# Layer 1's weight tiles fetched two by two: 1 MB transfers with 8192 B a partition in place of 512 KB with 4096 B

## The reference, cut to what matters

```python
def trunk_layer(x, start_pos, conv_buf, pool_buf, k_buf, v_buf, norm_g, w_in, ..., w_out):
    h = rms_norm(x, norm_g)
    proj = jnp.einsum('btd,de->bte', h, w_in)                 # 1024 -> 3200 columns
    a_val, a_glu, a_gate, b_val, b_gate, q, k, v, c_gate = jnp.split(proj, cuts, axis=-1)
    u = a_val * jax.nn.sigmoid(a_glu)
    c = layer_norm(causal_dwconv(concat(conv_buf, u), conv_w, conv_b), ln_g, ln_b)   # width 31
    ya = jax.nn.silu(c) * jax.nn.silu(a_gate)
    yb = multiscale_pool(concat(pool_buf, b_val), ...) * jax.nn.silu(b_gate)
    q, k = rope(rms_norm(q), pos), rope(rms_norm(k), pos)
    kk, vv = concat(k_buf, k), concat(v_buf, v)
    yc = dilated_attention(q, kk, vv, ...) * jax.nn.silu(c_gate)
    new_k, new_v = kk[:, -n_keep:], vv[:, -n_keep:]           # the cache, moved by one position
    return x + concat(ya, yb, yc) @ w_out, new_conv, new_pool, new_k, new_v
```

## Time and profile before

| | us |
|---|---|
| three runs | 398.08, 400.06, 397.24 |
| profiled execution, its own time | 398.96 |
| its span, first to last instruction | 397.1 |
| TensorE busy | 343.2 (86%) |
| VectorE busy | 232.3 (58%) |
| ScalarE busy | 100.1 (25%) |
| moved by DMA | 157.73 MB, mean 397 GB/s |

### The profile page before, as it was taken

One profiled execution on the slowest core, in us unless ns is written; L12 is line 12 of the kernel. 1 busy time (PEld: TensorE's weight loads), 2 busy tenths in 40 slices (PEclk: granted clock), 3 DMA queues, 4 the chain that ended last, 5 costly groups with the idle time before them and its releaser, 6 DMA issues.

```text
span 397.1 us, 4745 instructions
## 1 busy us (share of the span) xinstructions
PE 343.2 (86%) x1550; PEld 270.0 (68%) x1550; DVE 232.3 (58%) x530; ACT 100.1 (25%) x237; POOL 58.5 (15%) x110
## 2 busy tenths in 40 slices
PE   3897799998879859989958999999979867989990
PEld 2676578886557646578847888888747644658880
DVE  2603769759975996431013489978985997540110
ACT  4300013542523122411011011453352222230011
POOL 4007740003400011044001320000600002000000
PEclk9999989999969898999996999999978998989997
DMA  8999999999999999999999999999999999999982
GB/s 300 422 414 402 419 417 403 419 421 414 420 419 417 420 415 401 409 413 416 411 404 415 417 418 409 421 421 417 421 419 417 416 386 355 376 396 384 389 346 87
DMA packets 44329, 157.73 MB, mean 397 GB/s; under 512 B 6988, under 2 KB 20116, under 8 KB 44306
## 3 DMA queue, kind: packets, MB, share of 16 engines
q0 software_dynamic: 14624, 88.25, 54.5%
q10 hardware_dynamic: 14420, 41.52, 26.4%
q1 hardware_dynamic: 15262, 27.67, 18.7%
HBM read 140.23 MB, written 104.46 MB: 616 GB/s over the span
## 4 chain that ended last, share of the span: by engine, by line
PE 50%; DVE 14%; SPq 12%; DMA 10%; issue 5%; ACTq 4%; ACT 4%; DVEq 0%
PE pj L704 24%; PE pj L847 14%; SPq L491 11%; DMA kg<-in_cache_k_win 10%; DVE yc L1307 3%; PE psc L776 3%; PE ptr L622 3%; DVE ssc L1251 2%; ACTq L471 1%; PE ps L824 1%; ACTq L885 1%; DVE spsum_pad L1277 1%; DVE tok L1245 1%; DVE sc L1213 1%; PE ps L830 1%
## 5 line engine op out<-in xcount | busy, mean ns | idle before, releaser
L704 PE MATMUL pj<-hT,wt 128*128 128x264 f32 x800 | 195.5, 403 | 7.4 <-DVE hT L1162 5.0
L704 PEld LDWEIGHTS pj<-hT,wt 128*128 128x128 f32 x800 | 157.0, 200 | 39.7 <-issue 12.7
L1307 DVE SCALAR_TENSOR_TENSOR yc<-u_ext,par,yc 128x256 f32<-128x256 f32 x180 | 77.2, 480 | 3.8 <-DVE u_smp L1191 1.0
L847 PE MATMUL pj<-mix,wt 128*128 128x264 f32 x256 | 61.1, 395 | 0.0
L847 PEld LDWEIGHTS pj<-mix,wt 128*128 128x128 f32 x256 | 49.2, 195 | 8.4
L611 POOL DMA_DIRECT2D out<-in_cache_v_win x48 | 26.2, 553 | 143.3 <-issue 143.3
L1377 DVE TENSOR_TENSOR xT<-xT,pj 128x264 f32<-128x264 f32 x16 | 6.9, 430 | 55.2 <-PE pj L847 55.2
L611 POOL DMA_DIRECT2D out<-in_cache_k_win x48 | 26.4, 557 | 82.0 <-issue 82.0
L965 ACT ACTIVATE ex<-pj 128x264 f32<-128x264 f32 x22 | 8.6, 390 | 77.1 <-PE pj L704 44.0
L1245 DVE TENSOR_TENSOR tok<-kg,qb 128x1536 f32<-128x1536 f32 x10 | 17.6, 1758 | 4.2 <-DMA kg<-in_cache_k_win 3.7
L1189 DVE SCALAR_TENSOR_TENSOR u_ext<-ex,pj 128x256 f32<-128x256 f32 x6 | 2.5, 421 | 29.9 <-ACT ex L965 29.9
(11 more groups left out here) (187 smaller groups left out, 334.8 us busy)
## 6 DMA issues: line engine op xcount, KB each, us to landing
wt<-in_w_tiles ACTq DMA_DIRECT2D x62, 512.0 KB, 32.3
out<-in_cache_k_win POOLq DMA_DIRECT2D x24, 1080.0 KB, 44.4
out<-in_cache_v_win POOLq DMA_DIRECT2D x24, 1080.0 KB, 81.3
out<-in_cache_k_win POOLq DMA_DIRECT2D x8, 1200.0 KB, 72.0
out<-in_cache_v_win POOLq DMA_DIRECT2D x8, 1200.0 KB, 89.3
out<-in_cache_k_win POOLq DMA_DIRECT2D x16, 432.0 KB, 64.2
out<-in_cache_v_win POOLq DMA_DIRECT2D x16, 432.0 KB, 87.3
kg<-in_cache_k_win SPq DMA_DIRECT2D x32, 144.0 KB, 33.5
```

Of the source, the lines that this page charges most:

```text
L704: last = nc.tensor.matmul(pj[n % RING][:, 0:T], wt[:, g % WRING, k, :], hT[:, k, :], start=(k == 0), stop=(k == KD - 1))
L847: last = nc.tensor.matmul(pj[n % RING][:, 0:T], wt[:, g % WRING, k, :], mix[:, k, :], start=(k == 0), stop=(k == KD - 1))
L1307: last = V.scalar_tensor_tensor(out=yc[:, t, 0:SEQ], in0=x_w, scalar=par[:, ROW_CW + w * CT + t:ROW_CW + w * CT + t + 1], in1=yc[:, t, 0:S ...
```

## The change: single tiles up to the first of layer 1, pairs behind it

Tiles 34 to 65 lie in memory as 16 pairs, each partition's two rows of 4096 B side by side. One transfer fills two neighbouring slots of the ring with pieces of 8192 B. ACT issues it where it issued the odd tile, so the even tile of a pair is asked for one step later than before, and the even step issues nothing. TensorE waits for the even slot's semaphore for both tiles. SBUF, the schedules and the arithmetic stay.

```diff
+PAIRED_FROM = 34
+assert PAIRED_FROM % 2 == WRING % 2 == DEPTH * NRING % 2 == 0
...
+PAIR_BYTES = 2 * KD * P * 4
...
-    tiles = np.stack(cols, axis=1).reshape(DEPTH, NRING, KD, P, P)
-    return tiles.transpose(0, 1, 3, 2, 4).reshape(DEPTH, NRING, P, KD * P)
+    tiles = np.stack(cols, axis=1).reshape(DEPTH * NRING, KD, P, P).transpose(0, 2, 1, 3).reshape(DEPTH * NRING, P, KD * P)
+    pairs = tiles[PAIRED_FROM:].reshape(-1, 2, P, KD * P).transpose(0, 2, 1, 3).reshape(-1, P, 2 * KD * P)
+    return tiles[:PAIRED_FROM], pairs
...
         def tile_of(g):
-            return wt[:, g % WRING, :, :].rearrange("p k c -> p (k c)"), ins["w_tiles"][g // NRING, g % NRING], w_in[g % WRING]
+            if g < PAIRED_FROM:
+                return wt[:, g % WRING, :, :].rearrange("p k c -> p (k c)"), ins["w_tiles"][g], w_in[g % WRING]
+            return wt[:, g % WRING:g % WRING + 2, :, :].rearrange("p t k c -> p (t k c)"), ins["w_pairs"][(g - PAIRED_FROM) // 2], w_in[g % WRING]
+
+        def tile_landed(g):
+            g -= g % 2 if g >= PAIRED_FROM else 0
+            return w_in[g % WRING], 16 * (g // WRING + 1)
...
-                        pe.wait_ge(w_in[g % WRING], 16 * (g // WRING + 1))
+                        pe.wait_ge(*tile_landed(g))
...
             def next_tile(g):
-                if g < DEPTH * NRING:
+                if g < PAIRED_FROM:
                     buf, src, landed = tile_of(g)
                     act.dma_start(buf, src).then_inc(landed, 16)
+                elif g < DEPTH * NRING and g % 2:
+                    buf, src, landed = tile_of(g - 1)
+                    act.dma_start(buf, src, max_dma_last_dim=PAIR_BYTES).then_inc(landed, 16)
```

More of the change, by code:

```diff
@@ L1400 @@
     arrays, ins = {}, {}
-    a = np.ascontiguousarray(weight_tiles(inputs["w_in"], inputs["w_out"]))
-    arrays["in_w_tiles"] = a
-    ins["w_tiles"] = nc.dram_tensor("in_w_tiles", a.shape, F32, kind="ExternalInput").ap()
-    for name in _INS:
-        a = np.ascontiguousarray(inputs[name])
+    tiles, pairs = weight_tiles(inputs["w_in"], inputs["w_out"])
+    for name, a in (("w_tiles", tiles), ("w_pairs", pairs), *((name, inputs[name]) for name in _INS)):
+        a = np.ascontiguousarray(a)
         arrays[f"in_{name}"] = a
```

## The result

The changed kernel takes 403.89 us (median of 6 runs, 401.28 to 405.09), the kernel before, run beside it, 398.34 us. The ratio is 1.0124, 95% interval [1.0083, 1.0165]. A repeat on another chip gave 1.0132 [1.0085, 1.0178], the kernel before against itself there 0.9992 [0.9971, 1.0012]. The forecast was 399.1 in a range of 394.8 to 402.4; 403.89 lies above it, and the loss is 5.5 us where 1.0 was forecast. The profiled execution took 403.92 us.

The account below looks back on a forecast made before the run. Bound by full DMA engines and layer 1's key product, the end by TensorE's chain and slowest engines: border -2.9, keys' wait +5.3, further ahead -0.7 make +1.7, taken as +1.0: 399.1 us, range 394.8 to 402.4.

Parts of the forecast that it names:

- The border (-2.9): Between layers 0 and 1: without the tile issue behind the last square, TensorE starts layer 1 2.9 us earlier.
- Equal turns, larger pieces, SP the loser: DMA queues take equal packet turns, so ACT's 8192 B pieces gain share and SP's queue loses 24%, 0.74 MB.
- The rival in which the turns don't grow: Queue turns are cut by bytes, so only the border changes: 396.5 to 398 us, chance 7%.
- The 1.3 us: On the DMA engines: larger pieces move ACT's 16.8 MB more cheaply, saving 1.3 us at most.
- 16 transfers fewer: ACT's issues: 16 fewer at 0.34 us, 5.4 in all, mostly covered; a skill rule's 32 us applies only if exposed.
- The keys' delay (9 us, at most 10.8): Layer 1's key gather lands 9 us later, so its product starts at 272.2, 2.4 us late.
- the 0.74 of my bound: SP's queue by 263 us: 0.74 MB lost to ACT's, which puts the key gather up to 10.8 us later.
- as forecast (0.7): From layer 1's key product to the first `wout` step: TensorE being further ahead saves up to 0.7 us.
- Only part of the chain's delay shows: At the end: of +1.7 us on TensorE's work, only +1.0 shows in the time.
- I let the two cancel: At the tail: 1.3 us less from cheaper bytes against 0.7 us more from slower stores and copies, counted as zero.
- the last bytes come at 396.6 either way: At the end: the slowest engines' last bytes land at 396.6 us with or without the change.
- The rival "slower": At layer 1's key product: keys 10.8 us late, start +4.2, so 402.3 us, 405 with the clock; chance 15%.

Follow-up runs that it names:

- experiments 1 and 3: The second of these: the kernel before with tile 46 issued behind layer 1's first eviction, not behind layer 0's last square; 0.9994 of the kernel before.
- experiment 1: The changed kernel with its pairs kept but their pieces put back from 8192 B to 4096 B; 0.9991 of the kernel before.
- experiment 4: The kernel before with the first product on layer 1's keys done four times more on DVE; 1.0036 of the kernel before.
- experiment 9: The changed kernel without POOL's last three copies (2.7 MB, rows missing in the output); 0.998 of the kernel before.
- experiments 7 and 8: Layer 1's key gather cut to one slot a transfer: in the kernel before 0.9861, in the changed kernel 0.9922, both against the kernel before.
- experiment 5: The kernel before with tile 46 behind layer 1's first eviction and POOL's last six copies (5.4 MB) issued by ACT; 1.0286 of the kernel before.

## Why the prediction was wrong

- **The border (-2.9): right.** It gave 2.8 us, and TensorE's clock came back sooner on top. DVE was ready for the keys 6.1 us sooner: 2.1 are layer 0's scatter, 2.8 the border's, 1.2 came behind it. By experiments 1 and 3 the gain hangs on short stores; with pieces of 4096 B they took longer than the 4.48 us that I had called the worst.
- **Equal turns, larger pieces, SP the loser: right.** 8192 B is one turn. The rival in which the turns don't grow is refuted by the counts, and experiment 1 shows that the piece is the cause. ACT's queue did move its bytes a little cheaper (10.00 MB with a share of 42.0% are 25.7 GB/s an engine, 25.1 before), but the total didn't rise: 414 GB/s before and after. The 1.3 us did not come.
- **16 transfers fewer: worth nothing.** Experiment 1 has the 16 fewer transfers and small pieces, and takes 0.9991. (The 2.0 us a DMA stand on the Trainium skill's page "DMA: Bandwidth & Descriptors" in the section "Anatomy of one DMA — SWDGE (gpsimd) path", not in the one that the prediction names; that path is POOL's, and these transfers are ACT's.)
- **The keys' delay (9 us, at most 10.8): too small.** It was 13.3, and 14.2 in the repeat. SP lost 0.62 MB in 205 to 263 us, less than the 0.74 of my bound (the prediction's 24% are SP's part of what the others give up; of its own 3.99 MB, 0.74 are 19%). But I divided by its old rate of 69 GB/s when the rest came at the lower one (3.37 MB in 58 us, 58 GB/s): 0.62 MB are 10.7 us at that. And its slower queue let it issue its second group of gathers from 209.1 on instead of 205.3. The product came at 276.4, not at 272.2, and was 6.5 us late, not 2.4. The stretch behind it took 84.0 us, 0.6 less than before, as forecast (0.7).
- **Only part of the chain's delay shows: right**, by experiment 4: 7.2 us on DVE cost 1.4 (0.36%). It is why the late product alone is no explanation.
- **"I let the two cancel": this step failed, and with it "the last bytes come at 396.6 either way".** It priced the weights' early leaving at 15 us of stores and copies, 20 GB/s lower, 0.7 us, and set a gain of 1.3 against it. The last value store landed at 401.6. 1.3 MB less were moved from 280 to 340 us, and at 379 GB/s that is 3.4 us; over the whole span the repeat of the changed kernel was 2.2 MB behind by 340 us (135.8 against 138.0), 0.7 of it from 160 to 200 us, where its pairs begin. That is 5 to 6 us of work at the end, and the end was the bytes' (experiment 9). The row for it was there: before, the slices after 320 us stand at 355 to 396 and those ahead of it at 416 to 421. From 320 to 340 us before, without tiles, the rate is 365 GB/s, some 50 below the slices ahead of it and not 20, and I had not asked what a stall of DVE does to ACT's requests.
- **The size.** Of the 1.2 to 1.3%, pairs cost 0.6 with no wait for keys (experiments 7 and 8). The rest goes with the wait: it stops ACT's requests when ACT's queue is already empty, and it brings the chain to 398.3 (395.46, and 2.8 to the end as in experiment 4), short of the bytes' end at 402. That this is how the rest arises is argued, not shown: no run stops ACT's requests by themselves with pairs, and experiments 7 and 8 also read 2.7 MB less. The rival "slower" had 402.3 by the chain alone. Its sign was right, but by experiment 4 the chain alone is the smaller part, so a time near its number is luck.

**What stays open** is why the rate falls. Shown is this: I took windows of 4 us (20 to 376 us, all 16 profiles) in which copies and ACT's stores move 160 GB/s or more, and grouped them by that rate in steps of 40. Those with tile loads move 406 to 413 GB/s in all, in every group. Those without move 342, 369, 398 and 387 in the groups from 240, 280, 320 and 360 on. That is an average. In single microseconds of the changed kernel copies and gathers alone reach 412 to 432 (276 to 280 us) and, 2 us later, 261. Three queues of stores don't mend it (experiment 5). Whether it is the writing, the addresses or something else that is slow there, no run tells, since none measured one of them by itself.

## What to carry over

Where the DMA engines are full and turns are equal, the size of a queue's pieces is its priority: enlarge only those of the queue that others wait for. Here the sum of all queues was some 38 GB/s higher, on average, with tile loads beside the copies than without (412 against 374 in the windows above). So bringing loads forward left a slower rest; price it as bytes not moved, at the rate that the profile shows where there are no loads. And ask of every new wait whose requests stop with it.

## What I had not expected of the hardware

- A packet of POOL's that takes 291 ns took up to 944 ns in the dip at 282 to 285 us, and SP's packets stretched as well: one of 1536 B took 779 ns, where those of 6144 B mostly take 234. The engines still count as busy (9 in every slice); only GB/s shows it.
- `max_dma_last_dim` cut ACT's pieces (4096 and 2048 B) but not POOL's: 1853 packets of 10.64 MB from 205 to 263 us with the edit, 1856 of 10.61 without it.
- Half the size of piece on ACT's last ten tiles cost 14.6 us, by way of ScalarE's issues: a store that had taken 0.32 us to issue took 7.25.
